# Attention rounds dealt in another way, and three gate tiles of the layer-norm stage computed inside the rounds of the first three head pairs

## The chip, the cores and the metric

The kernel runs on one core of a Trainium2 chip. The metric is device time in microseconds, lower is better; a run's time is that of the whole program.

## What is computed

One inference step of a hybrid encoder layer (depth 1) for two groups that share weights: 1024 new frames of a prompt and 64 new frames of a running stream, 1088 tokens in all, width 1024.

```python
h = rmsnorm(x)
q, k, v, glu_a, glu_b, g_attn, g_conv = split(h @ w_in + b_in)      # 1024 -> 3*512 + 2*512 + 2*1024
q, k = rmsnorm per head (8 heads x 64)
# stick-breaking attention, strictly causal, keys: own frames (+ 2048 cached ones for the sample group)
A[t,s] = sigmoid(z_ts) * prod_{s<j<t} (1 - sigmoid(z_tj));  a = (A @ v) @ w_attn_out
u = glu_a * sigmoid(glu_b);  c = causal depthwise conv of u, width 31, 512 channels
c = silu(layernorm(c)) @ w_conv_out + b_conv_out
x = x + (sigmoid(g_attn) * a + sigmoid(g_conv) * c) @ w_out
x = x + conv_ffn(rmsnorm(x));  y = rmsnorm(x)
```

Keys, values and the convolutions' last rows are outputs too. All of it is in fp32; each product is made of three passes, both factors being split into a high and a low part (`split_passes`).

## The kernel before, in words

PE (TensorE) does the matmuls, ACT (ScalarE) activations and copies out of PSUM, DVE (VectorE) elementwise work, POOL (GpSimd) some subtractions, SP issues the DMAs. Every engine works through its own queue in order; semaphores tie the queues together. The stages are blocks, and at the end of a block the engines meet.

Stage 1 makes `hhi` and `hlo`, the normalised input, and the projections of head pair 0.

Stage 2 is a window for each of the four head pairs p, each of 17 rounds r (0 to 16). A round treats two units of attention: up to 512 keys for 128 queries of one head (rounds 0 to 11; widths 128, 256, 384, 512, then 128 and 512, 256 and 512, 384 and 512, 512 and 512), and from round 12 the 64 sample queries against own and cached keys. A unit goes through the engines so:
- PE: `scores(p, r)` into one of two banks `ZB`;
- ACT: `sig`, two sigmoids per unit, into `sn` (2 buffers) and `sg` (4 buffers). It waits until the scan of the unit two before has read `sn`, and until PE's transposes of the unit four before have read `sg`;
- DVE: `weights`, a scan over `sn` and a product into `sg`;
- PE in round r+2: `w_transposes`; ACT: `w_evac`; PE in round r+3: `outputs`.

Between these pieces PE works on projections for the next pair, in half-jobs ("halves") of 12 matmuls (four of eight contraction tiles, three passes): 9 jobs of the next pair's q, k, v (`qkv_half`, numbers t = 0 to 8, 384 columns) and 6 jobs of its GLU inputs (`ab_half`, 364 columns). The jobs alternate between the two banks `PJ`; a job may start when the job two before it has been evacuated: q, k, v by DVE (`qkv_evac`, semaphore `qkv_ev`), GLU inputs by ACT (`b_evac`, a sigmoid into `sigb`) and DVE (`a_evac`). In each round PE issues scores, outputs of round r-3, masks, all halves but the last, the transposes of round r-2, the last half. The weights of the jobs lie in five slots of `whi` and `wlo`: a DMA fills `wraw`, ACT converts (`slot_hi`), DVE subtracts (`slot_lo`). In the last pair the jobs are 15 chunks of gate tiles 0 to 4 (`gate_half`, evacuated by ACT in `gate_evac`).

DVE also does the 31 taps of the depthwise convolution of pair p (`tap`), dealt over the rounds by the table `TAPS`, one list for each pair; in a round DVE does the evacuation first, then the weights, then `slot_lo` and norms, then its taps. Tap 0 waits until `c_sb` of the pair before has been stored.

Stage 3 computes the other 11 of 16 gate tiles (33 chunk jobs of 24 matmuls on PE, `gate_job`), and beside them the layer norm of the convolution: channel sums, squares, roots, reciprocals, sigmoids, then `chi` (ACT) and `clo` (POOL). ACT and POOL also prepare the weights that follow (`PREP3`, `make_hi`, `make_lo`). Stage 4 reads the gates back from HBM and mixes both branches; it first needs `ohi` and `olo`, made from `oraw`. Stage 5 is the feed-forward network.

Of the kernel before, what the change touches and what calls it, by code (L numbers as in the profile page):

```python
# [15 lines left out]
F32 = mybir.dt.float32  # L16
F32R = mybir.dt.float32r
BF16 = mybir.dt.bfloat16
ALU = mybir.AluOpType
# [3 lines left out]
P = 128  # L23
# [60 lines left out]
def build(nc, a, o, scr):  # L84

    ctx = ExitStack()
    with ctx:
# [27 lines left out]

        def gate_col(g):

            return 3 * AW + 2 * CC + D * (g % 2) + P * (g // 2)
# [24 lines left out]
        gate_ev, gate_out2, c_out, o_out = sem("gate_ev"), sem("gate_out2"), sem("c_out"), sem("o_out")  # L143
        PJ, XB = bank[0:2], bank[2:6]

# [52 lines left out]
        def qkv_evac(dve, p, t):  # L198
# [7 lines left out]
            dve.tensor_tensor(stage[:, t, :], PJ[t % 2][:, 0:3 * P], bqkv[:, :], ALU.add).then_inc(qkv_ev, 1)  # L206

        def qkv_half(pe, p, t, half):
            if half == 0:
                if t == 0:  # L210
                    pe.wait_ge(lo_done, 5 * p + 3)
                if t >= 2:
# [5 lines left out]
            for k in range(4 * half, 4 * half + 4):  # L218
                ws = slice(P * k, P * k + P)
                for n, (x, w) in enumerate(split_passes(hhi, hlo, whi, wlo)):  # L220
                    mm = pe.matmul(PJ[t % 2][:, 0:3 * P], x[:, k, tok], w[:, 0:3, ws],  # L221
# [226 lines left out]
        with ExitStack() as c2:  # L448
# [31 lines left out]
            AB_ROUND = {9: (0, 1), 10: (2,), 11: (3,), 12: (4,), 13: (5,), 14: (6,), 15: (7,), 16: (8, 9, 10, 11)}  # L480
            GATE_ROUND = {r: (2 * r, 2 * r + 1) if r < 13 else (13 + r,) for r in range(NR)}
            B_EVAC_ROUND, A_EVAC_ROUND = {10: 0, 14: 1}, {12: 0, 16: 1}
            NORM_ROUND = {11: 0, 12: 1, 13: 2}
            HI_ROUND, LO_ROUND = {9: 0, 10: 1, 13: 2}, {10: 0, 12: 1, 14: 2}

            def dealt(carried, own):
                out = [[] for _ in range(NR)]
                for p in range(PAIRS):
# [3 lines left out]
                    for r in range(NR):  # L492
# [17 lines left out]
            def _(sp):  # L510
# [41 lines left out]
                def window(p):  # L552
                    load_bias(sp, p + 1)
                    for x in range(2):
                        load_ab(sp, x, p + 1)
# [11 lines left out]
                    load_past(p, 3, "k")  # L567
# [40 lines left out]
            def _(act):  # L608
                def b_evac(p, c):
# [3 lines left out]
                    if later(need):  # L613
                        act.wait_ge(a_ev, need)
                    act.wait_ge(bias_b_done, p + 1)
                    act.activation(sigb[:, 0:c1_ - c0], PJ[(9 + 2 * c) % 2][:, 0:c1_ - c0], ACT.Sigmoid,
                                   bias=bias_b[:, :]).then_inc(b_ev, 1)

# [1477 lines left out]
```

## Time and profile before

| | us |
|---|---|
| median of 3 runs | 1704.54 (1704.46 to 1704.71) |
| profiled execution, its own time | 1699.73 |
| its span | 1697.8 |
| stage 2, windows of the four pairs | 112.6, 116.4, 115.7, 110.0 |
| stage 3 | 137.3 |

The profile comes from one execution, whose time is 4.8 us under the median. Its rows name an engine, a line of the code, and the tile written and those read (out<-in). PE is TensorE's matmul, PEld its weight load, which overlaps. Matmuls are pipelined: one of 384 columns lasts 0.33 us, but the next starts 0.17 us after it, so starts tell more than lengths. An idle time stands in front of the instruction that ended it, with the one that released it. The granted clock is a share of 2.4 GHz.

### The profile page before, as it was taken

The numbers are of one execution on the slowest core, as the hardware profiler recorded it, in microseconds if no ns is written. First come the engines' busy times: TensorE is split into PE (matmuls) and PEld (weight loads), VectorE is DVE, ScalarE is ACT, GpSimd is POOL, SyncE is SP. The second block draws the span as 40 slices with busy tenths as digits, with TensorE's granted clock in tenths as the row PEclk, the third lists the DMA queues.
The fourth block names the chain that finished last, engine by engine and source line by source line (L and its number), as shares of the span: only waits on it lengthen the run. The fifth ranks groups of instructions, "written<-read, shape, count | busy, mean of one in ns | idle before, by whom it ended". The sixth has DMA issues, their size and how long they took to land. (4 is left out here: it accounts for less than half of the span.)

```text
span 1697.8 us, 26678 instructions
## 1 busy us (share of the span) xinstructions
PE 1647.2 (97%) x9802; PEld 1524.0 (90%) x9802; DVE 1131.3 (67%) x1628; ACT 609.3 (36%) x1541; POOL 102.7 (6%) x71
## 2 busy tenths in 40 slices
PE   7999999998999999999999999999999999999998
PEld 6997887887987999999989998999989999998996
DVE  5479799799796233444477665676656666665677
ACT  5446446446444234211154131322313122131224
POOL 0000000000000114332320000000000000000000
PEclk9999999999999999999999999999999999999999
DMA  5330320402313422723312020211102111020102
GB/s 187 84 79 20 93 58 20 126 26 58 92 69 122 157 78 93 242 87 90 102 38 87 26 63 13 62 44 43 49 25 62 33 42 61 25 62 17 57 13 108
DMA packets 145879, 119.42 MB, mean 70 GB/s; under 512 B 6763, under 2 KB 130127, under 8 KB 145800
## 3 DMA queue, kind: packets, MB, share of 16 engines
q1 hardware_dynamic: 145800, 118.35, 22.6%
q8 instruction: 51, 0.84, 0.2%
q14 instruction: 28, 0.23, 0.0%
HBM read 95.83 MB, written 22.50 MB: 70 GB/s over the span
## 5 line engine op out<-in xcount | busy, mean ns | idle before, releaser
L1638 PE MATMUL bank<-h2hi,whi 128*128 128x364 f32 (+1 forms) x1056 | 347.7, 329 | 2.1 <-PEq L1644 2.1
L1638 PE MATMUL bank<-h2lo,whi 128*128 128x364 f32 (+1 forms) x1056 | 347.6, 329 | 0.0
L1638 PE MATMUL bank<-h2hi,wlo 128*128 128x364 f32 (+1 forms) x1056 | 347.5, 329 | 0.0
L1423 DVE TENSOR_TENSOR x<-bank,x 128x512 f32<-128x512 f32 x270 | 181.1, 689 | 166.6 <-PE bank L1413 161.7
L1638 PEld LDWEIGHTS bank<-h2hi,whi 128*128 128x128 f32 x1056 | 199.0, 188 | 2.7 <-issue 2.3
L1638 PEld LDWEIGHTS bank<-h2lo,whi 128*128 128x128 f32 x1056 | 199.0, 188 | 0.4
L1638 PEld LDWEIGHTS bank<-h2hi,wlo 128*128 128x128 f32 x1056 | 199.0, 188 | 0.0
L815 DVE SCALAR_TENSOR_TENSOR c_sb<-u,dww,c_sb 128x1118 f32<-128x1118 f32 x120 | 165.8, 1382 | 2.7
L1413 PE MATMUL bank<-whi,mhi 128*128 128x512 f32 x342 | 133.7, 391 | 2.4 <-PEq L1433 1.2
L1413 PE MATMUL bank<-whi,mlo 128*128 128x512 f32 x342 | 133.3, 390 | 0.0
L1413 PE MATMUL bank<-wlo,mhi 128*128 128x512 f32 x342 | 133.3, 390 | 0.0
L1855 ACT ACTIVATE gsig<-cvg 128x364 f32<-128x364 f32 (+1 forms) x66 | 33.4, 506 | 273.9 <-DVE cvg L1947 273.9
L1163 ACT ACTIVATE whi<-wraw 128x1024 fp32r<-128x1024 f32 x77 | 80.7, 1054 | 89.9 <-PE bank L1413 59.7
L667 ACT ACTIVATE sn<-bank 128x512 f32<-128x512 f32 (+3 forms) x116 | 58.3, 502 | 151.1 <-PE bank L1010 131.0
L221 PE MATMUL bank<-whi,hhi 128*128 128x384 f32 x288 | 103.6, 360 | 5.6 <-DVE stage L206 3.3
L1838 ACT ACTIVATE up<-bank 128x364 f32<-128x364 f32 (+2 forms) x176 | 64.2, 391 | 111.5 <-PE bank L1638 109.4
L221 PE MATMUL bank<-whi,hlo 128*128 128x384 f32 x288 | 99.0, 344 | 0.0
L221 PE MATMUL bank<-wlo,hhi 128*128 128x384 f32 x288 | 98.7, 343 | 0.0
L1363 PE MATMUL bank<-hhi,whi 128*128 128x364 f32 (+1 forms) x264 | 88.0, 333 | 0.9 <-PEq L448 0.9
L1363 PE MATMUL bank<-hlo,whi 128*128 128x364 f32 (+1 forms) x264 | 86.7, 328 | 0.0
L1363 PE MATMUL bank<-hhi,wlo 128*128 128x364 f32 (+1 forms) x264 | 86.7, 328 | 0.0
L1941 DVE TENSOR_SCALAR cvv<-up,ffw,prm 128x364 f32<-128x364 f32 (+1 forms) x66 | 31.0, 470 | 77.0 <-ACT up L1838 77.0
(206 smaller groups left out, 3398.5 us busy)
## 6 DMA issues: line engine op xcount, KB each, us to landing
wraw<-in_w_up SPq DMA_DIRECT2D x88, 256.0 KB, 3.2
wraw<-in_w_in SPq DMA_DIRECT2D x30, 512.0 KB, 5.0
wraw<-in_w_down SPq DMA_DIRECT2D x44, 256.0 KB, 2.8
scr_gate<-gst SPq DMA_DIRECT2D x11, 544.0 KB, 4.4
gch<-scr_gate SPq DMA_DIRECT2D x16, 364.0 KB, 3.7
xt<-in_x_prompt SPq DMA_DIRECT2D x8, 512.0 KB, 5.2
kpast<-in_cache_sb_k SPq DMA_DIRECT2D x16, 256.0 KB, 5.3
wraw<-in_w_out SPq DMA_DIRECT2D x16, 256.0 KB, 2.8
```

Of the source, the lines that this page charges most:

```text
L221: mm = pe.matmul(PJ[t % 2][:, 0:3 * P], x[:, k, tok], w[:, 0:3, ws], start=(k == 0 and n == 0), stop=(k == KT - 1 and n == 2))
L667: act.activation(sn[:, s % 2, 512 - n:512], z, ACT.Sigmoid, scale=-DH ** -0.5)
L815: dve.scalar_tensor_tensor(out=c_sb[:, :], in0=x, scalar=w, in1=c_sb[:, :], op0=ALU.mult, op1=ALU.add).then_inc(tap_done, 1)
L1163: act.activation(dst, wraw[:, parity, :], ACT.Copy).then_inc(sems[1], 1)
L1363: mm = pe.matmul(bank[j % 4][:, 0:c1_ - c0], w[:, g % 5, ws], x[:, k, c0:c1_], start=(k == 0 and i == 0), stop=(k == KT - 1 and i == 2))
L1413: mm = pe.matmul(bank[banks[d % len(banks)]][:, :], x[:, k, TOK[t]:TOK[t] + P], w[:, 512 * half:512 * half + 512], start=(k == 0 and n == ...
L1423: dve.tensor_tensor(y, bank[banks[d % len(banks)]][:, :], y, ALU.add).then_inc(down_ev, 1)
L1638: mm = pe.matmul(bank[(3 * tau + c) % 4][:, 0:c1_ - c0], w[:, ws], x[:, k, c0:c1_], start=(k == 0 and n == 0), stop=(k == KT - 1 and n == 2))
L1838: ins = act.activation(up[:, x, x0 + sh + 2:x1_ + sh + 2], bank[(3 * tau + c) % 4][:, x0 - c0:x1_ - c0], ACT.Copy)
L1855: act.activation(gsig[:, (3 * j + c) % 2, 0:n], cvg[:, c, 0:n], ACT.Sigmoid).then_inc(gsig_done, 1)
L1941: dve.tensor_scalar(dst, src[:, n0 + 2:n1 + 2], w(2), prm[:, ds(PRM_FDB + tile, 1)], ALU.mult, ALU.add).then_inc(c2_done, 1)
```

## The change

- Gate tiles 13, 14 and 15 leave stage 3. Each becomes three chunk jobs (`gate_chunk_half`) inside the window of pair 0, 1 and 2. Stage 3 keeps 8 tiles, 24 jobs.
- The order of jobs in these windows is now q, k, v jobs 0 to 4, gate chunk 0, 5, 6, chunk 1, 7, 8, chunk 2, then the six GLU jobs (`Q_AT`, `GW_AT`). Rounds 3 to 8 hold three halves instead of two, rounds 9 to 11 one instead of two, one and one, rounds 12 and 13 two. In the rounds with cached keys the first half stands ahead of the scores.
- The gate weights use slot 4 and `wraw[0]`; the GLU weights of slot 4 come later, converted in round 9, subtracted in round 10. ACT evacuates gate chunks in rounds 5, 7 and 9, behind `attention(p, r)`, into `sigb`, from which SP stores them.
- DVE's taps are dealt anew, some evacuations come behind the weights, `a_evac`, `b_evac` and the slots move by a round or two.
- The last pair uses the same deal: one half in rounds 9 to 11, three in round 16.
- Stage 3: roots, sigmoids and `chi` move forward by jobs, seven weights are prepared in place of ten, the last behind the last job.

```diff
+        NG = 2 * KT
+        NG3 = NG - 3 - 5
...
+        Q_AT, GW_AT = (0, 1, 2, 3, 4, 6, 7, 9, 10), (5, 8, 11)
...
+                if p and t in (6, 8):
+                    pe.wait_ge(gw_ev, 3 * (p - 1) + t // 2 - 2)
+                elif p and t in (5, 7):
+                    pe.wait_ge(qkv_ev, NT * p + t)
+                elif t >= 2:
                     pe.wait_ge(qkv_ev, NT * p + t - 1)
...
-            AB_ROUND = {9: (0, 1), 10: (2,), 11: (3,), 12: (4,), 13: (5,), 14: (6,), 15: (7,), 16: (8, 9, 10, 11)}
-            GATE_ROUND = {r: (2 * r, 2 * r + 1) if r < 13 else (13 + r,) for r in range(NR)}
-            B_EVAC_ROUND, A_EVAC_ROUND = {10: 0, 14: 1}, {12: 0, 16: 1}
+            LATE_ROUND = {9: (0,), 10: (1,), 11: (2,), 12: (3, 4), 13: (5, 6), 14: (7,), 15: (8,), 16: (9, 10, 11)}
+            B_EVAC_ROUND, A_EVAC_ROUND = {11: 0, 14: 1}, {13: 0, 15: 1}
+            GATE_EVAC_ROUND = {**{n + 1: n for n in range(9)}, 11: 9, 12: 10, 13: 11, 15: 12}
             NORM_ROUND = {11: 0, 12: 1, 13: 2}
-            HI_ROUND, LO_ROUND = {9: 0, 10: 1, 13: 2}, {10: 0, 12: 1, 14: 2}
+            HI_ROUND, LO_ROUND = {11: 0, 12: 1, 14: 2}, {12: 0, 13: 1, 15: 2}
+            GW_FIRST = NG - 3
...
-                         [[3, 2, 1, 1, 3, 2, 2, 2, 3, 2, 0, 0, 0, 0, 1, 3, 6],
-                          [0, 3, 3, 1, 3, 3, 2, 2, 2, 2, 1, 0, 0, 0, 1, 3, 5],
-                          [0, 3, 3, 2, 3, 2, 3, 2, 2, 2, 0, 0, 0, 0, 1, 3, 5],
-                          [0, 3, 3, 3, 3, 3, 2, 2, 3, 1, 3, 3, 2, 0, 0, 0, 0]])
+                         [[4, 1, 1, 2, 4, 4, 4, 3, 4, 1, 0, 0, 1, 1, 1, 0, 0],
+                          [0, 0, 4, 4, 4, 4, 4, 4, 4, 1, 1, 0, 1, 0, 0, 0, 0],
+                          [0, 0, 4, 4, 4, 4, 4, 4, 4, 1, 1, 0, 1, 0, 0, 0, 0],
+                          [0, 0, 4, 4, 4, 3, 2, 2, 3, 0, 1, 1, 3, 3, 1, 0, 0]])
...
-                    for x in range(2):
-                        load_ab(sp, x, p + 1)
+                    load_ab(sp, 0, p + 1)
+                    sp.wait_ge(lo_done, 5 * p + 8)
+                    sp.dma_start(wraw[:, 0, :].rearrange("p (k n) -> p k n", k=KT),
+                                 w_in[:, :, ds(gate_col(GW_FIRST + p), P)]).then_inc(gw_in, 16)
...
+                    sp.wait_ge(gw_lo, p + 1)
+                    load_ab(sp, 1, p + 1)
+                    for c, (c0, c1_) in enumerate(CHUNKS):
+                        sp.wait_ge(gw_ev, 3 * p + c + 1)
+                        sp.dma_start(scr["gate"][GW_FIRST + p][:, c0:c1_], sigb[:, 0:c1_ - c0]).then_inc(gw_out, 16)
                     for s in range(3):
+                        if s == 2:
+                            load_past(p, 3, "k")
                         if p < PAIRS - 2:
                             load_qkv(sp, s, p + 2)
                         else:
                             load_slot(sp, s, 4, gate_col(s))
-                    load_past(p, 3, "k")
...
+                def gate_chunk(p, c):
+                    c0, c1_ = CHUNKS[c]
+                    act.wait_ge(gw_ready, 3 * p + c + 1)
+                    if c or p:
+                        act.wait_ge(gw_out, 16 * (3 * p + c))
+                    if c == 0:
+                        act.wait_ge(a_ev, 3 * p + 3)
+                    act.activation(sigb[:, 0:c1_ - c0], PJ[GW_AT[c] % 2][:, 0:c1_ - c0], ACT.Sigmoid,
+                                   bias=gate_bias(GW_FIRST + p)).then_inc(gw_ev, 1)
...
                     for r in range(NR):
                         attention(p, r)
-                        if r in (0, 1):
-                            slot_hi(act, 3 + r, p + 1)
+                        if r == 0:
+                            slot_hi(act, 3, p + 1)
+                        if r == 1:
+                            gate_weights_hi(p)
+                        if r in (5, 7, 9):
+                            gate_chunk(p, (r - 5) // 2)
+                        if r == 9:
+                            act.wait_ge(gw_ready, 3 * p + 3)
+                            slot_hi(act, 4, p + 1)
...
-                        if 1 <= r <= 13:
-                            gate_evac(r - 1)
-                        if r == 15:
-                            gate_evac(13)
+                        if r in GATE_EVAC_ROUND:
+                            gate_evac(GATE_EVAC_ROUND[r])
...
-                        if 1 <= r <= NT:
+                        if r in (1, 2, 3, 4, 6, 8):
                             qkv_evac(dve, p + 1, r - 1)
                         if r in A_EVAC_ROUND:
                             a_evac(p + 1, A_EVAC_ROUND[r])
                         for u in units_of(r):
                             weights(p, u)
+                        if r in (4, 6, 8):
+                            qkv_evac(dve, p + 1, r)
                         if r == 0:
                             next_bias(p + 1)
-                        if r in (2, 3):
-                            slot_lo(dve, 1 + r, p + 1)
+                        if r == 2:
+                            slot_lo(dve, 3, p + 1)
+                        if r == 3:
+                            dve.wait_ge(gw_hi, p + 1)
+                            dve.tensor_tensor(wlo[:, 4, :], wraw[:, 0, :], whi[:, 4, :].bitcast(F32),
+                                              ALU.subtract).then_inc(gw_lo, 1)
+                        if r == 10:
...
-                        if n == 0:
-                            pe.wait_ge(lo_done, 5 * p + 5)
                         if n < 2:
-                            pe.wait_ge(qkv_ev, NT * p + 8 + n)
+                            pe.wait_ge(lo_done, 5 * p + 4 + n)
+                        if n == 1 and p:
+                            pe.wait_ge(gw_ev, 3 * p)
+                        elif n < 2:
+                            pe.wait_ge(qkv_ev, NT * p + (9 if p else 8 + n))
...
+                def gate_chunk_half(p, c, half):
+                    c0, c1_ = CHUNKS[c]
+                    if half == 0:
+                        if c == 0:
+                            pe.wait_ge(gw_lo, p + 1)
+                        pe.wait_ge(qkv_ev, NT * (p + 1) + 4 + 2 * c)
...
+                    job, half = h // 2, h % 2
+                    if job in Q_AT:
+                        qkv_half(pe, p + 1, Q_AT.index(job), half)
+                    elif job in GW_AT:
+                        gate_chunk_half(p, GW_AT.index(job), half)
                     else:
-                        ab_half(p + 1, (h - 2 * NT) // 2, h % 2)
+                        ab_half(p + 1, job - NT - 3, half)
 
                 def halves_of(p, r):
                     if p == PAIRS - 1:
-                        return GATE_ROUND[r]
-                    return (2 * r, 2 * r + 1) if r < NT else tuple(2 * NT + h for h in AB_ROUND[r])
+                        return (2 * r, 2 * r + 1) if r < NT else tuple(2 * NT + h for h in LATE_ROUND[r])
+                    if r < NT:
+                        return (2 * r, 2 * r + 1) if r < 3 else tuple(range(3 * r - 3, 3 * r))
+                    return tuple(2 * NT + 6 + h for h in LATE_ROUND[r])
 
                 def window(p):
                     for r in range(NR - 1):
                         halves = halves_of(p, r)
+                        if pasts_of(r):
+                            half_(p, halves[0])
...
                     for r in range(NR - 1):
                         halves = halves_of(p, r)
+                        if pasts_of(r):
+                            half_(p, halves[0])
+                            halves = halves[1:]
                         if r < len(ROUNDS):
                             scores(p, r)
...
                     halves = halves_of(p, NR - 1)
                     for x, h in enumerate(halves):
-                        if x == len(halves) - 1:
+                        if x == 2:
                             outputs(p, NR - 3)
+                            if p < PAIRS - 1:
+                                qk_transposes(p + 1, 4)
+                                qk_transposes(p + 1, 5)
                         half_(p, h)
-                        if x < len(halves) - 1:
+                        if x < 2 and p < PAIRS - 1:
                             for n in (2 * x, 2 * x + 1):
...
-            PREP3 = [(g % 5, 3 * (g - 9)) for g in range(10, NG)] + [(1, 21), (2, 24), (3, 27), (4, 30)]
+            PREP3 = [(g % 5, 3 * (g - 9)) for g in range(10, NG3 + 5)] + [(3, 12), (4, 15), (1, 21), (2, 24)]
+            PREP_AT3 = {2: 0, 5: 1, 8: 2, 12: 3, 15: 4, 21: 5, 23: 6}
...
-                    if n in (6, 7, 8):
-                        c_lo(n - 6)
+                    if n == 4:
+                        c_lo(0)
+                        c_lo(1)
+                    if n == 5:
+                        c_lo(2)
...
-                    if j == 15:
+                    if j == 13:
                         roots()
-                    if j in (18, 22, 26):
-                        sigmoids((j - 18) // 4)
-                    if j in (21, 25, 29):
-                        c_hi((j - 21) // 4)
...
+                    if j in (14, 17, 20):
+                        sigmoids((j - 14) // 3)
+                    if j in (16, 19, 22):
+                        c_hi((j - 16) // 3)
+                    if j in PREP_AT3:
+                        n = PREP_AT3[j]
                         act.wait_ge(g_ready, PREP3[n][1])
                         make_hi(act, raw3, n // 2 + 1, n, n % 2, whi[:, PREP3[n][0], :])
...
```

## Rows read from the trace of the kernel before

**Rows 1.** The page, part 1: busy us, share of the span, instructions.
```profile
PE 1647.2 (97%) x9802; PEld 1524.0 (90%) x9802; DVE 1131.3 (67%) x1628; ACT 609.3 (36%) x1541; POOL 102.7 (6%) x71
```

**Rows 2.** By stage: stretch, length, busy PE, PEld, DVE, ACT, POOL; clock, DMA, GB/s.
```profile
91.30:203.90 112.60, 107.73 (x779) 94.60 (x778) 102.53 (x115) 61.50 (x189) 0.00 (x0) 1.00 0.18 51
203.90:320.30 116.40, 109.45 (x778) 96.10 (x778) 102.43 (x115) 61.88 (x189) 0.00 (x0) 0.99 0.22 62
320.30:436.00 115.70, 109.42 (x777) 96.09 (x776) 102.42 (x115) 62.04 (x189) 0.00 (x0) 0.99 0.22 63
436.00:546.00 110.00, 104.52 (x759) 91.01 (x759) 92.16 (x97) 52.99 (x118) 0.02 (x1) 1.00 0.29 92
546.00:683.30 137.30, 136.38 (x812) 134.53 (x813) 42.88 (x36) 48.81 (x69) 37.89 (x15) 1.00 0.34 117
```

**Rows 3.** Waits of PE, 85 to 546 us: who waited for whom, total, times, longest.
```profile
PE bank L960 <- ACT wT L676: 9.6, 8, 2.7
PE bank L999 <- ACT kTpast L683: 6.0, 12, 0.8
PE bank L221 <- DVE stage L206: 3.3, 2, 1.9
```

**Rows 4.** The same view without a filter on the engine.
```profile
ACT sn L667 <- PE bank L1010: 131.0, 47, 4.6
```

**Rows 5.** Timeline of PE, first matmul of stage 4; in brackets the idle time.
```profile
683.31 0.41 PE L1598 MATMUL bank<-chi,whi 128*128 128x364 f32 x1 [0.91 <-PEq L1170]
```

**Rows 6.** Timeline of ACT, the last weight conversion of stage 3.
```profile
678.92 1.05 ACT L1163 ACTIVATE whi<-wraw 128x1024 fp32r<-128x1024 f32 x1
```

**Rows 7.** Timeline of POOL, the subtraction that follows it.
```profile
680.04 2.41 POOL L1167 TENSOR_TENSOR wlo<-wraw,whi 128x1024 fp32r<-128x1024 f32 x1 [4.32 <-ACT whi L1163]
```

**Rows 8.** Landing times of the DMAs that write `oraw`.
```profile
DMA to landing us min/median/max: 4.4/7.2/9.9
```

**Rows 9.** Timeline of ACT, last pair, round 5 of the attention.
```profile
468.52 0.60 ACT L667 ACTIVATE sn<-bank 128x512 f32<-128x512 f32 x1 [4.67 <-DVE run L845]
...
470.45 1.12 ACT L676 ACTIVATE wT<-bank 128x512 f32<-128x512 f32 x2
471.41 0.61 ACT L708 ACTIVATE stage<-bank,prm 128x364 f32<-128x364 f32 x1
```

**Rows 10.** Timeline of DVE, second pair, rounds 2 and 3.
```profile
220.58 0.95 DVE L845 TENSOR_TENSOR_SCAN run<-sn 128x385 f32<-128x385 f32 x1
...
223.50 1.22 DVE L178 TENSOR_TENSOR wlo<-wraw,whi 128x1024 fp32r<-128x1024 f32 x1
224.64 4.22 DVE L815 SCALAR_TENSOR_TENSOR c_sb<-u,dww,c_sb 128x1118 f32<-128x1118 f32 x3
228.77 0.55 DVE L206 TENSOR_TENSOR stage<-bank,bqkv 128x384 f32<-128x384 f32 x1
229.24 1.22 DVE L845 TENSOR_TENSOR_SCAN run<-sn 128x513 f32<-128x513 f32 x1
...
232.97 1.22 DVE L178 TENSOR_TENSOR wlo<-wraw,whi 128x1024 fp32r<-128x1024 f32 x1
```

**Rows 11.** Timeline of PE, second pair, round 5 up to the start of round 6.
```profile
236.03 1.14 PE L979 MATMUL bank<-kT,qT 64*128 64x256 f32 x8
...
240.09 1.04 PE L1010 MATMUL bank<-ident,sg 128*128 128x128 f32 x8
240.88 0.42 PE L221 MATMUL bank<-whi,hhi 128*128 128x384 f32 x1
...
243.17 0.71 PE L979 MATMUL bank<-kT,qT 64*128 64x128 f32 x8
```

**Rows 12.** Timeline of PE after its 1.9 us wait for DVE, second pair.
```profile
230.20 0.52 PE L221 MATMUL bank<-wlo,hhi 128*128 128x384 f32 x1
...
232.75 1.23 PE L1010 MATMUL bank<-ident,sg 128*128 128x128 f32 x6
```

**Rows 13.** Columns as in rows 2 (granted clock third from last), that stretch alone.
```profile
230.00:233.00 3.00, 3.00 (x12) 2.90 (x12) 2.93 (x5) 0.42 (x4) 0.00 (x0) 0.53 0.00 0
```

More of the change, by code:

```diff
@@ L205, in qkv_evac @@
                     dve.wait_ge(wt_ready, NWT * (p - 1) + 6)
-            dve.tensor_tensor(stage[:, t, :], PJ[t % 2][:, 0:3 * P], bqkv[:, :], ALU.add).then_inc(qkv_ev, 1)
+            dve.tensor_tensor(stage[:, t, :], pj_qkv(p, t)[:, 0:3 * P], bqkv[:, :], ALU.add).then_inc(qkv_ev, 1)
         def qkv_half(pe, p, t, half):
@@ L1054, in sample_outputs @@
                     mm.then_inc(av_done, 1)
+                def gate_chunk_half(p, c, half):
[4 more added lines that the diff above has]
+                        pe.wait_ge(qkv_ev, NT * (p + 1) + 4 + 2 * c)
+                    for k in range(4 * half, 4 * half + 4):
+                        ws = slice(P * k, P * k + P)
+                        for i, (w, x) in enumerate(split_passes(whi, wlo, hhi, hlo)):
+                            mm = pe.matmul(PJ[GW_AT[c] % 2][:, 0:c1_ - c0], w[:, 4, ws], x[:, k, c0:c1_],
+                                           start=(k == 0 and i == 0), stop=(k == KT - 1 and i == 2))
+                    if half:
+                        mm.then_inc(gw_ready, 1)
                 def half_(p, h):
@@ L1080, in window @@
                             w_transposes(p, u)
-                        half_(p, halves[-1])
+                        for h in halves[-1:]:
+                            half_(p, h)
                         for j in pasts_of(r + 1):
@@ L1201, in _ @@
                 n = 0
-                for g in range(NG - 5):
-                    while n < len(PREP3) and n < g + 3:
-                        if n < NG - 10:
+                for g in range(NG3):
+                    while n < len(PREP3) and n < g + 2:
+                        if n < NP3:
                             send_raw(sp, raw3, n, n % 2, k_halves(w_in, gate_col(10 + n)))
                         else:
-                            send_out_weights(sp, raw3, n, n % 2, n - (NG - 10), 0)
+                            send_out_weights(sp, raw3, n, n % 2, OUT_ORDER[n - NP3], 0)
                         n += 1
-                    if g == NG - 6:
+                    if g == NG3 - 1:
                         sp.wait_ge(clo_done, 3)
@@ L1283, in _ @@
                 slot_hi(act, 4, 5)
-                for j in range(3 * (NG - 5)):
+                for j in range(3 * NG3):
                     gate_evac(j)
@@ L1370, in channel_mean @@
                     return pe.matmul(bank[4 + c][:, 0:CHUNKS[c][1] - CHUNKS[c][0]], ones[:, :], src, start=True, stop=True)
-                for j in range(3 * (NG - 5)):
+                for j in range(3 * NG3):
                     gate_job(j)
```

43 lines of the change are left out of this document (25 added, 18 removed).

## Prediction

> **What bounds the kernel now.** I read the page's busy table first: PE works 97% of the span [rows 1]. Then the busy time by stage, cut where each head pair's first score matmul starts: the four pair windows last 112.6, 116.4, 115.7 and 110.0 us, the gate and layer-norm stage 137.3 [rows 2]. PE is busy 94% of a pair window and 99% of that stage. So PE's queue sets the time nearly everywhere. Moving matmuls from one stage to another doesn't shorten anything by itself. The change can win only what PE now idles in the pair windows, and it must not add waits there. Third, who waited for whom: over all four pairs PE waited 9.6 us for ACT's copies ahead of the cache transposes, 6.0 us for the transposed cache keys, 3.3 us for DVE's projection evacuation [rows 3]; with smaller items 22 us in all. That is the purse. The opposite direction is the row to look at longest: ACT waited 131.0 us in 47 waits for PE's transposes of the weights [rows 4]. ACT is not busy there, but it is chained to PE: the sigmoids of round r overwrite buffers that PE's transposes of round r-2 must have read, and PE issues these late in round r.
>
> **Part 1, nine gate jobs move.** A job is 24 matmuls. Stage 3 runs 812 matmuls in 137.3 us [rows 2], 0.167 us each, so a job is 4.0 us. Stage 3 falls by 9 x 4.0 = 36.0; the pair windows rise by nine jobs, 36.3 with the slower first matmul after each switch.
>
> **Part 2, the end of stage 3.** Before the change PE's last gate job is followed by an evacuation and a barrier, and stage 4 starts at 683.31 after 0.91 us of idle [rows 5]; the last weight is converted one job earlier and hidden: ACT's conversion 1.05, POOL's subtraction 2.41 [rows 6, 7]. After the change the last of the seven weights is converted on ACT behind the last gate evacuation: 0.6 + 1.05, then 2.41 on POOL, then the barrier, about 4.4 us after PE's last job instead of 1.1: +3.3. The third `clo` part (3.3 us on POOL) also ends only about 1.4 us after PE's last job, so SP's two loads of `oraw` are issued there, land 4.4 us later at best [rows 8], and ACT's `ohi` copies wait for them: about 1.9 us more in front of the second job of stage 4. The layer-norm chain in between (means, squares, roots, reciprocals) keeps two jobs of slack. Stage 3 with its hand-over: -36.0 + 3.3 + 1.9 = **-30.8 us**.
>
> **Part 3, waits on ACT's order.** In rounds 5 and 7 of pairs 0 to 2 the third half-job belongs to projections 6 and 8, which write the PSUM bank that gate chunks 0 and 1 left. It waits for `gw_ev`, and ACT evacuates the chunk only behind `attention(p, r)` of the same round. That call starts with four sigmoids that wait for PE's transposes of that very round, and these stand immediately ahead of the waiting half-job. So PE must sit through four sigmoids, two copies and the evacuation. The last pair has exactly this sequence: first sigmoid at 468.52, copies at 470.45, gate evacuation 471.41 plus 0.61 [rows 9]: 3.5 us, 3.6 with the hand-overs. Round 7 has an `o_sb` copy more (0.5). Cost 3.6 + 4.1 = 7.7 us per pair, 23 us for three. Nothing can hide it, since PE's queue is in order; behind it stand the next round's scores, hence ACT's and DVE's next work.
>
> **Part 4, DVE's deadlines.** DVE is busy 102.4 of 116.4 us in a pair [rows 2] and gets one subtraction more. A tap costs 1.38 (three from 224.64 to 228.77), an evacuation 0.47, a subtraction 1.14, two 384-wide weight units 2.9, two 512-wide ones 3.7 [rows 10]. A PE round with two halves is 7.1 us [rows 11]; a third half adds 2.1 to 2.2. The new deal puts no taps in rounds 0 and 1 of pairs 1 and 2 and four in each of rounds 2 to 8. Walk of pair 1, us from the start of round 2, each line a sum of those prices:
> Round 2: DVE can start its scans at 4.1 (behind PE's scores, one half, transposes and the first sigmoids); 2.9 + 1.1 + 5.5 ends at 13.7. PE enters round 3 at 5.5.
> Round 3: PE wants its third half (projection 4) at 11.8; it needs evacuation 2, which DVE does first in its round 3: 14.2. Stall 2.4 (now 1.9 a round later [rows 3]; the cause there is a tap waiting for a DMA, which the new deal removes). DVE: 0.5 + 3.7 + 1.1 + 5.5, ends 24.6.
> Round 4: PE wants gate chunk 0 at 19.8; its bank needs evacuation 3, done 25.1. Stall 5.3. Round 5 starts at 30.
> Round 5: the ACT-order stall, 3.6. Round 6: evacuation 5, stall 1.3. Round 7: ACT order, 4.1. Round 8: evacuation 7, about 0.8.
> Rounds 9 to 11 now hold one half each, 4.6 to 5.3 us of PE, while DVE comes out of round 8 some 8 us late with 5 to 6 us of work per round: about 2.5 in round 10 (sigmoids behind DVE's scan) and 3.0 in round 11 (slot 4's low part, now made in DVE's round 10, only just before PE needs it); these replace the present 2.7 there. Round 15: 1.2, since the half that covered ACT's last weight copy now stands ahead of the scores.
> New stalls 24; three gate jobs 12; against them the present stall with its slow clock (3.7), 2.7, and some 1.5 from half-jobs ahead of the cache scores and 1 in small items fall away: 24 + 12 - 9 = **+27** for pair 1, and as much for pair 2. Pair 0 has one and two taps in rounds 2 and 3: no stall in round 3, 3.5 in round 4, the rest as before, but also no present stall to lose: **+26**. Pair 3 has no extra jobs; its taps (4, 4, 4 in rounds 2 to 4 against 3, 3, 3) put DVE later, and rounds 9 to 11 give PE less to do meanwhile: walked in the same way 11.2 us of idle for the 5.5 of now, **+5.5**. Pairs: +86 (26 + 27 + 27.5 + 5.5), the third rounded up for its shorter window now.
> The DMAs moved along: the gate weights and three chunk stores per pair on SP have two rounds between them, 15 us for transfers of a few us. The load for slot 0 of the next pair now waits for the late subtraction of round 10 and reaches ACT just in time; bound 0 to 2 us per pair, I take 0.
>
> **Part 5, the clock.** After the 1.9 us wait [rows 3] the granted clock was 0.53 over the next stretch [rows 13], that is the lower level, 1.2 GHz: eight matmuls stand 0.32 us apart instead of 0.17 (230.20 to 232.75), six transposes take 1.23 where eight took 1.04 [rows 11, 12]: 1.2 + 0.4, with the edges 1.7 us lost. The third pair shows the same; the 2.7 us waits of round 11 in three pairs show none. So two of five. Nine stalls of over 3 us are new (rounds 4, 5, 7): 0 to 9 x 1.7 = 15 us, I take two fifths, **+6**. The Trainium skill (TensorE: Matmul & The Clock Gate, section What's actually happening) says that the throttled state is the default and activity releases it. By that each long stall would pay, and the sum would be 9 us higher; the trace agrees only in part.
>
> **Sum.** -30.8 + 86 + 6 = +61. The profiled execution took 1699.7 us (span 1697.8), 4.8 under the median of the runs; against the median 1704.5 + 61 = **1766 us**.
>
> **Rivals.** (A) The sum, 1740 to 1787 with its bounds (clock, slot load, a few us per pair): chance 0.72.
> (B) DVE's deadlines don't bite, because the stalls of part 3 let it catch up each time; only part 3 remains: -30.8 + 36.3 + 23 - 7 (present round-4 stalls) - 4.5 = +17, 1722, spread 1712 to 1739. Against it: round 4 comes before the first such stall, and DVE's 21 us of work in rounds 2 and 3 against 14 of PE's. Chance 0.15.
> (C) The other side: the new jobs fall into PE's present idle time. It decides only if neither part 3 nor part 4 holds, that is, if ACT and DVE are early at every bank. Then -30.8 + 36.3 - 22 = -16.5, 1688 (1680 to 1708 if the purse is only partly emptied). For it: ACT is busy only half of each window [rows 2]. Against: rows 4, idle ACT is not free ACT. Chance 0.05, of which 0.02 within 0.2%.
> (D) The window doesn't grow: weight loads fill only 96.1 of its 116.4 us [rows 2], so 20 us would be open for 12 us of jobs. Then only -30.8: 1674. Against it: transposes and scores follow each other without idle, at 0.79 us for eight [rows 11]; the rest of the load time is theirs. Chance 0.02. The Trainium skill (Perfetto Trace Analysis, section Identifying the Most-Contended Engine) has this as its rule, that PE's headroom is read from weight-load share and not matmul share; it speaks for D.
> (E) Worse: every long stall runs into half clock and the slow PE delays ACT and DVE in turn, +85 to +100, about 1795: 0.06.
> Likeliest time 1766. The range 1716 to 1787 leaves out C, D and E. A change of 0.2% (3.4 us) is about what can be measured. Faster 0.05, within 0.02, slower 0.93.
>
> **What would show it.** Right: stage 3 about 105 us; windows near 139, 143, 143, 115; PE waiting for ACT's gate evacuation (`sigb`) six times for 3.6 to 4.1 us, and for DVE's `stage` evacuation in round 4 of three pairs for 3 to 5; more stretches at half clock. Wrong: pair windows below 130, or no wait on `sigb`, which would break part 3; waits on `stage` missing would make it B.

## The result and the profile after

The changed kernel takes 1772.91 us (median of 4 runs, 1772.42 to 1775.44), beside 1704.5 for the kernel before in the same runs. The ratio of the means is 1.041, interval 1.0396 to 1.0424. The forecast was 1766, with a range of 1716 to 1787. The profiled execution has a span of 1773.6 us, 75.8 more than before. Part 1 of the page, with the columns of rows 1:

```profile
PE 1671.9 (94%) x9802; PEld 1544.1 (87%) x9802; DVE 1129.6 (64%) x1631; ACT 607.2 (34%) x1541; POOL 94.5 (5%) x68
```

PE runs the same 9802 matmuls, yet is busy 25 us longer and idle 51 us longer. Where that lies is told by the stages, cut as in rows 2, with the same columns:

```profile
91.70:237.10 145.40, 128.30 (x851) 113.39 (x850) 103.94 (x116) 63.22 (x193) 0.00 (x0) 0.93 0.16 45
237.10:385.80 148.70, 127.31 (x849) 113.57 (x849) 104.30 (x116) 63.72 (x194) 0.00 (x0) 0.94 0.20 56
385.80:533.40 147.60, 128.79 (x851) 113.50 (x850) 104.29 (x116) 63.75 (x194) 0.00 (x0) 0.93 0.20 57
533.40:652.20 118.80, 105.56 (x760) 91.96 (x759) 92.35 (x97) 53.73 (x119) 0.07 (x1) 0.99 0.29 87
652.20:757.00 104.80, 100.51 (x596) 98.63 (x597) 35.68 (x36) 40.98 (x57) 29.63 (x12) 1.00 0.34 118
```

The pair windows grew by 32.8, 32.3, 31.9 and 8.8 us, 105.8 in all, and stage 3 shrank by 32.5. Each of the first three windows has 72 matmuls more, which are worth 12.1 us; the other 20 us of each are no work. The granted clock fell from 0.99 or 1.00 to 0.93 or 0.94. The waits of PE from 85 to 652 us, as in rows 3:

```profile
PE bank L237 <- ACT sigb L658: 20.8, 6, 3.7
PE bank L1037 <- ACT sg L710: 16.1, 9, 2.8
PE bank L1123 <- DVE stage L218: 12.4, 4, 3.8
PE bank L1110 <- ACT wT L718: 5.9, 4, 1.5
PE bank L978 <- DVE wlo L190: 5.1, 3, 2.8
PE bank L237 <- DVE stage L218: 4.5, 2, 2.2
```

L237 is a matmul of a projection, L1123 of a gate chunk, L1037 a score, L978 an A or B half-job, L1110 an output from cached values. In idle times of more than 0.15 us PE has stood still for 70 us up to the end of stage 3 instead of 23, +47. So of the 105.8 us, 36.3 are the moved matmuls, 47 are waits, and 22.5 are left. They lie in how fast PE goes after a wait. The second pair, round 4, timeline of PE:

```profile
268.47 0.34 PE L237 MATMUL bank<-whi,hlo 128*128 128x384 f32 x1
272.52 0.64 PE L1123 MATMUL bank<-hhi,whi 128*128 128x364 f32 x1 [3.71 <-DVE stage L218]
272.96 0.51 PE L1123 MATMUL bank<-hlo,whi 128*128 128x364 f32 x1
273.27 0.51 PE L1123 MATMUL bank<-hhi,wlo 128*128 128x364 f32 x1
```

and the stretch behind it, columns as above:

```profile
272.60:278.60 6.00, 6.00 (x22) 5.92 (x23) 0.83 (x3) 1.15 (x5) 0.00 (x0) 0.50 0.00 0
```

PE stands 3.71 us, then starts a matmul each 0.30 us instead of 0.17, at a granted clock of 0.50, that is 1.2 GHz. In stage 2 the records show 61.4 us at this level, against 6.8 before: 54.6 more, and the 22.5 us left over are 0.41 us for each of them. This is a remainder, not a measurement. It can be held against another reading of the same trace: 5.0 of the 61.4 us lie inside waits, and if PE works at half speed in the other 56.4, it loses 28.2 us there, against 3.4 before. That is 24.8 more, an estimate near the 22.5.

### The profile page after: what moved, and what is told of

Its sections match the earlier page's. It is cut to its first block and busy times, and to the rows that moved or that the text cites. A ratio compares the mean times of both kernels' runs of the same rounds, so it can differ in the third digit from the quotient of the medians.

```text
span 1773.6 us, 26704 instructions
## 1 busy us (share of the span) xinstructions
PE 1671.9 (94%) x9802; PEld 1544.1 (87%) x9802; DVE 1129.6 (64%) x1631; ACT 607.2 (34%) x1541; POOL 94.5 (5%) x68
## 5 line engine op out<-in xcount | busy, mean ns | idle before, releaser
L237 PE MATMUL bank<-whi,hhi 128*128 128x384 f32 x288 | 106.0, 368 | 27.6 <-ACT sigb L658 20.8
L893 DVE TENSOR_TENSOR_SCAN run<-sn 128x129 f32<-128x129 f32 (+3 forms) x68 | 54.3, 799 | 77.1 <-ACT sg L710 77.1
L237 PE MATMUL bank<-whi,hlo 128*128 128x384 f32 x288 | 101.6, 353 | 0.0
L237 PE MATMUL bank<-wlo,hhi 128*128 128x384 f32 x288 | 101.3, 352 | 0.0
L237 PEld LDWEIGHTS bank<-whi,hhi 128*128 128x128 f32 x288 | 57.7, 201 | 31.6 <-ACT sigb L658 22.3
L1499 PEld LDWEIGHTS bank<-whi,mhi 128*128 128x128 f32 x342 | 64.2, 188 | 15.8 <-issue 3.1
```

The costliest lines, as they stand in the source:

```text
L237: mm = pe.matmul(pj_qkv(p, t)[:, 0:3 * P], x[:, k, tok], w[:, 0:3, ws], start=(k == 0 and n == 0), stop=(k == KT - 1 and n == 2))
L893: dve.tensor_tensor_scan(run[:, s % 3, 512 - n:513][:, ::-1], x, x, init, ALU.mult, ALU.min).then_inc(scan_done, 1)
L1499: mm = pe.matmul(bank[banks[d % len(banks)]][:, :], x[:, k, TOK[t]:TOK[t] + P], w[:, 512 * half:512 * half + 512], start=(k == 0 and n == ...
```

## Experiments

All compare with the kernel before on the same chip (1702 to 1704 us) and show the ratio to it; the changed kernel's is 1.041. Experiments 1 to 4, 5 to 8, 9 to 11, and 12 ran on four different chips, so between these groups the ratios tell more than the microseconds.

**1 to 3: which engine holds PE up.** Theory A: each stall of the prediction is a term of its own. Theory B: DVE paces the stretch, and the wait for ACT only stands ahead of one for DVE. First, ACT takes the gate chunk ahead of the attention work:

```diff
                     for r in range(NR):
+                        if r in (5, 7, 9):
+                            gate_chunk(p, (r - 5) // 2)
                         attention(p, r)
...
-                        if r in (5, 7, 9):
-                            gate_chunk(p, (r - 5) // 2)
```

> The changed kernel (1772.9 us), with one edit: in rounds 5, 7 and 9 ScalarE evacuates the gate chunk ahead of the round's attention work instead of behind it. Theory A (each stall is its own term): the six waits of TensorE for sigb in rounds 5 and 7, 20.8 us in the changed kernel's profile, go, and the stretches at half clock behind them with them, some 7 us: about 1745 us. Theory B (VectorE, with four taps in each of rounds 2 to 8, paces the whole stretch, and the ScalarE wait only stands ahead of a VectorE wait that would come anyway): TensorE waits for stage or for w_done instead, in rounds 6 to 8, and at most 5 us are won: about 1768 us. Above 1757 is B, below is A.

Measured 1774.9 us, ratio 1.0428 (1.0402 to 1.0454): nothing won. PE's waits, 85 to 652 us:

```profile
PE bank L1123 <- DVE stage L218: 36.7, 9, 4.6
PE bank L1037 <- ACT sg L710: 14.0, 7, 2.8
PE bank L978 <- DVE wlo L190: 8.2, 3, 2.8
```

The 20.8 us for `sigb` in rounds 5 and 7 are gone, and the waits of the gate chunks for DVE rose from 12.4 in 4 to 36.7 in 9: beside round 4's 3.7 now 4.6 in round 6 and 3.0 to 4.5 in round 8. The waits moved one round on and changed their name. Second, DVE takes tiles 3, 5 and 7 behind the weights of the round that computes them, ahead of its four taps (5.5 us):

```diff
-                        if r in (1, 2, 3, 4, 6, 8):
+                        if r in (1, 2, 3):
                             qkv_evac(dve, p + 1, r - 1)
...
-                        if r in (4, 6, 8):
+                        if 3 <= r <= 8:
                             qkv_evac(dve, p + 1, r)
```

> The changed kernel, with one edit: in rounds 3 to 8 VectorE evacuates the projection tile of the round behind the round's running products and ahead of its taps, instead of tiles 3, 5 and 7 at the head of the next round. Theory A: the waits of TensorE for stage in round 4 (12.4 us in 4) shrink to under 2 us, the half clock behind them goes too, and the ScalarE waits of rounds 5 and 7 stay as they are: about 1756 us. Theory B: VectorE is merely handed its work in another order, its taps push the running products of the next round back, and TensorE meets ScalarE's and VectorE's lateness a round later: 1765 us or more.

Measured 1757.9 us, ratio 1.032 (1.029 to 1.035), as A said: the waits of round 4 went, the 20.8 us for `sigb` stayed. Third, both edits:

> The edits of the two experiments before it together. Theory A (independent terms): their gains add, some 28 + 16 us: about 1729 us. Theory B (one chain paced by VectorE): together hardly more than the better of the two: 1755 us or more. If the two together bring more than their sum, each had only moved the stall to the other engine.

Measured 1729.3 us, ratio 1.0162 (1.0133 to 1.0192): 43.7 us less than the changed kernel, where the edits alone gave nothing and 15. The waits for `sigb` are gone and those of the gate chunks for DVE's `stage` with them; what is left, 85 to 605 us:

```profile
PE bank L1037 <- ACT sg L710: 14.5, 9, 2.8
PE bank L237 <- DVE stage L218: 9.0, 5, 2.2
```

The time is the one that A forecast, but not by A's addition: the first edit alone had brought nothing, and brings 28.6 us once the second is in. That is the last sentence of the expectation. Round 4's wait was DVE's alone. In rounds 5 to 8 DVE's queue and ACT's order are two chains that end at nearly the same moment, and each alone suffices to hold PE. The stretches at half clock fell from 61.4 to 23.9 us with them.

**4: the last pair.** Its rounds, evacuations and taps are dealt as in the kernel before; in part:

```diff
-                        return (2 * r, 2 * r + 1) if r < NT else tuple(2 * NT + h for h in LATE_ROUND[r])
+                        return (2 * r, 2 * r + 1) if r < 13 else (13 + r,)
...
-                          [0, 0, 4, 4, 4, 3, 2, 2, 3, 0, 1, 1, 3, 3, 1, 0, 0]])
+                          [0, 3, 3, 3, 3, 3, 2, 2, 3, 1, 3, 3, 2, 0, 0, 0, 0]])
```

> The changed kernel with the last pair's rounds, evacuations and taps dealt as in the kernel before. The prediction put +5.5 us on the last pair; its stretch has since measured 118.8 us against 110.0. Theory A: all of the 8.8 us is the new deal of that pair: 1764 us. Theory B: part of it comes from the pair ahead (the carry-over of taps, the state of the clock) and stays: 1768 to 1772 us.

Measured 1767.6 us, ratio 1.038 (1.0352 to 1.0407). The window is 115.6 us: 3.2 of the 8.8 us came back. The time is close to B's, but the rest does not come from the pair ahead. Rounds 0 to 11 now take 73.8 us against 74.2 in the kernel before, and the pair's waits for sigmoids are 0.8 us instead of 8.5; but some 5 us of other waits stand in rounds 12 to 15, where this kernel, having one half-job in each, still put it ahead of the scores and left nothing behind the transposes. In experiment 8, which undoes that among other things, the window is 109.6.

**5: the clock.** Twenty matmuls of 384 columns are put ahead of the last half-job of rounds 4 and 5. In round 5 that is the half-job that waits. In round 4 it isn't: there the second of the three half-jobs waits, and the fillers stand behind that wait:

```diff
+                        if r in (4, 5) and p < PAIRS - 1:
+                            filler(p, r)
                         for h in halves[-1:]:
                             half_(p, h)
```

> The changed kernel plus 20 matmuls of 384 columns (some 3.4 us of work, results never read, into a bank that is free then) just ahead of the half-job that waits in rounds 4 and 5 of the first three pairs: TensorE works where it stood idle. If the half clock in the rounds behind those two waits comes from the standing still, the stretches at half clock in stage 2 (61 us in the profile of the changed kernel) shrink by a third or more and the time falls by 5 to 12 us, although 120 matmuls more are done: 1761 to 1768 us. If the clock falls for another reason, the filler only takes the place of the waits where they are at least as long, and lengthens the rest: 1773 to 1780 us.

Measured 1778.1 us, ratio 1.0441 (1.0427 to 1.0455): slower, in the range of the second reading. The half clock fell from 61.4 to 47.8 us, by 22%, where the first reading asked for a third. PE's waits, 80 to 655 us, then the second pair's round 4, with the fillers in its last row:

```profile
PE bank L1123 <- DVE stage L218: 15.0, 7, 3.7
PE bank L1037 <- ACT sg L710: 14.4, 8, 2.8
PE bank L237 <- ACT sigb L658: 11.2, 3, 3.7
```

```profile
273.30 0.64 PE L1123 MATMUL bank<-hhi,whi 128*128 128x364 f32 x1 [3.67 <-DVE stage L218]
...
276.66 0.82 PE L1068 MATMUL bank<-ident,sg 128*128 128x128 f32 x6
277.23 3.72 PE L1132 MATMUL bank<-hhi 128*128 128x384 f32 x20
```

In round 5 the fillers took the wait away in all three pairs, and no slow stretch lies there any more, where two of three had one. Instead a wait of 1.15 us for DVE stands in round 6 of each, where only pair 1 had one. In round 4 the wait of 3.7 us comes first and the fillers after it, so it could not shrink: those 60 matmuls were work for nothing. So 120 matmuls of 0.172 us cost 20.6 us, 11.5 us of waits went, and 13.6 us of half clock are worth 5.6 at 0.41. The sum is 3.5; the profiled span changed by 1.4, the median by 5.2. Half of the cost is the misplaced half, 10.3 us, so the run doesn't show whether fillers that stand only where PE waits would pay. In round 5 it does show a PE that doesn't stand still and keeps its clock.

**6: taps.** Only the taps are spread; the rows of pairs 1 and 2, and pair 0's in the same manner:

```diff
-                          [0, 0, 4, 4, 4, 4, 4, 4, 4, 1, 1, 0, 1, 0, 0, 0, 0],
+                          [0, 1, 2, 2, 3, 3, 3, 3, 3, 2, 0, 0, 0, 0, 1, 3, 5],
```

> The changed kernel with nothing but the taps of the first three pairs spread more evenly: at most three in a round, and eight of them in the last two rounds, where VectorE stands idle for 12 us. Theory A (independent terms): what TensorE waits for VectorE in rounds 3, 4, 8 and 10 goes (some 22 us of waits with 5 us of half clock), the ScalarE waits of rounds 5 and 7 stay: about 1747 us. Theory B (the two engines stand in for each other, as moving the ScalarE evacuation alone showed): the ScalarE waits remain whole and set the pace of rounds 5 to 8, so that only the waits of rounds 3, 4 and 10 go: about 1758 us.

Measured 1758.6 us, ratio 1.033 (1.0315 to 1.0344), the time of B, though not by all of its steps. The waits for `sigb` are 20.8 us to the digit. Those of round 3 are gone, those of round 10 are at most 1.1 us instead of 2.5; round 4's is 2.3 in pair 0 and still 3.6 in the others, since tile 3 is evacuated only at the head of DVE's round 4 there. And PE, now earlier in round 11, waits 4.2 us for `wlo`, slot 4's low part, in pairs 1 and 2.

**7: the kernel before, lightened.**

```diff
-                          [0, 3, 3, 1, 3, 3, 2, 2, 2, 2, 1, 0, 0, 0, 1, 3, 5],
-                          [0, 3, 3, 2, 3, 2, 3, 2, 2, 2, 0, 0, 0, 0, 1, 3, 5],
+                          [0, 2, 2, 1, 3, 3, 3, 3, 2, 2, 1, 0, 0, 0, 1, 3, 5],
+                          [0, 2, 2, 1, 3, 3, 3, 3, 2, 2, 1, 0, 0, 0, 1, 3, 5],
...
-                        if r == 10:
+                        if r == 11:
                             roots(p + 1)
...
-            NORM_ROUND = {11: 0, 12: 1, 13: 2}
+            NORM_ROUND = {12: 0, 13: 1, 14: 2}
```

> The kernel before, without any gate tile in the pairs, with two edits: one tap less in rounds 1 and 2 of pairs 1 and 2 (moved to rounds 5 and 6), and the square roots with the two table loads of ScalarE one round later, where it stands idle, the norms one round later with them. In its profile TensorE waits 9.6 us for wT evacuations (three of them 2.7 us, behind the square roots) and 3.3 us for stage tiles, with 6.8 us at half clock behind the latter. If both go: 12 to 15 us less, about 1690 us. If the waits are only passed on to the next round: 1698 to 1703 us.

Measured 1718.1 us, ratio 1.0083 (1.0069 to 1.0097): both expectations missed. Its first wait of PE, and SP's issues in the second pair:

```profile
PE bank L1052 <- DMA vpast<-in_cache_sb_v: 14.2, 3, 4.8
```

```profile
313.62 0.67 SPq L540 DMA_DIRECT2D out_v_sample<-stage  x1
314.35 1.40 SPq L531 DMA_DIRECT2D vpast<-in_cache_sb_v  x1
```

The stores of keys and values wait for the norms. Norms a round later put the load of past values behind them in SP's queue: its issue lies 104.4 us behind the start of the window (209.9), where it lay 100.0 behind it before, and PE waited 4.8 us for a transfer that takes 3.9. The kernel shows 27.3 us at half clock, 20.5 of them at these three.

**8: every cure.** Experiments 3, 4 and 6 together, tile 2 evacuated in its own round, the later roots of 7, and for the last pair:

```diff
-                        if pasts_of(r):
+                        if pasts_of(r) and p < PAIRS - 1:
                             half_(p, halves[0])
```

> The changed kernel with every cure at once: ScalarE evacuates the gate chunks first, VectorE evacuates each projection tile behind the running products of its own round, the taps are spread (at most three in a round), the square roots stand a round later, and the last pair is dealt as before, its half-jobs too. The gate tiles stay inside the pairs. By the sum, the 36 us of matmuls that are moved and the 36 us that stage 3 loses cancel, 5 us of hand-over and start of stage 4 remain, and 10 us of waits of the kernel before go with the square roots and the spread taps: about 1700 us. If the rounds that carry three half-jobs cost of their own more than their matmuls, it stays above 1710 us.

Measured 1733.9 us, ratio 1.0179 (1.0165 to 1.0193). The intervals of this and of experiment 3 overlap, so the further cures brought nothing, where the expectation was 1700 us. Two waits stand in the way: 15.3 us for `vpast`, again outside DVE and ACT, and 10.9 for `wlo`, which DVE makes.

**9 to 11: the queue.** Two edits to 8, of which the second alone is applied to 7; the third kernel is 8 with the first edit and the old roots:

```diff
-                        if r == 10:
+                        if r == 9:
                             slot_lo(dve, 4, p + 1)
...
-                    store_kv(p + 1)
                     for j in (2, 3):
                         load_past(p, j, "v")
+                    store_kv(p + 1)
                     store_o(p)
```

> The kernel with every cure (1733.9 us) and two edits: the low part of the A weights is made in round 9 instead of round 10, and SyncE issues the loads of the past values ahead of the stores of keys and values. Its profile shows TensorE waiting 15.3 us for vpast (three times 5) and 10.9 us for wlo (three times 3.6). Theory A (SyncE stands at the store, which waits for the norms that the later square roots pushed back, and the loads stand behind it): both waits go with most of the half clock behind them, 1704 us. Theory B (the transfers themselves are late, or the stores in their turn hold up the next pair's first evacuation): the waits move to the first rounds of the next pair, 1720 us or more.

> The kernel before with one tap less in rounds 1 and 2 and the later square roots (1718.1 us), and now the loads of the past values ahead of the stores of keys and values in SyncE's queue. Theory A: the 14.2 us of waits for vpast and the 20 us more of half clock go, and what remains is the gain that was forecast first: 1692 us. Theory B (the stores come late in their turn, or the square roots cost as much a round later): 1700 to 1706 us.

> As the first kernel of this group, but the square roots in round 10 and the order of SyncE's queue as they were in the changed kernel: gate tiles inside the pairs, evacuations early, taps spread, low part of the A weights in round 9, last pair as before. If the square roots and the queue are a wash, it is level with the first kernel, about 1705 us; if the later square roots are worth their 8 us, some 1712 us.

Measured 1716.7 (ratio 1.0095, 1.0080 to 1.0111), 1698.2 (0.9982, 0.9973 to 0.9991) and 1706.9 us (1.0029, 1.0017 to 1.0042). The first two lie between what their theories forecast. The third comes to the 1705 of its expectation, but is not level with the first kernel: it is 10 us below it. The waits for `vpast` are gone in the two in which SP's order changed and, but for 0.5 us, in the third, in which the norms are early again: either end of the mechanism removes them. The waits for `wlo` went with the earlier low part. In the first kernel these stand in their place:

```profile
PE bank L1017 <- ACT wT L718: 12.0, 11, 3.1
...
PE bank L237 <- issue: 4.5, 3, 2.1
```

The later square roots stand ahead of copies that the cache transposes need, and 2.1 us appear in the first rounds of each following pair, as theory B had it. In 10 too `wT` costs 9.5 us, as much as in rows 3. The roots in round 10 are the better place. The stages of experiment 11, the first three pairs and the last:

```profile
90.00:216.50 126.50, 121.07 (x851) 108.01 (x850) 104.00 (x116) 63.00 (x193) 0.00 (x0) 0.99 0.18 52
216.50:345.00 128.50, 120.81 (x851) 107.58 (x850) 104.04 (x116) 63.62 (x194) 0.00 (x0) 0.99 0.23 65
345.00:474.90 129.90, 121.93 (x851) 108.84 (x850) 104.19 (x117) 63.66 (x194) 0.00 (x0) 0.97 0.22 64
474.90:584.40 109.50, 104.39 (x759) 90.97 (x758) 92.29 (x98) 53.40 (x119) 0.00 (x0) 1.00 0.30 95
```

The gate tiles are still inside the pairs, with DVE as busy as in the changed kernel. The windows are those of rows 2 plus 12.1 us for the three jobs, to within 2.1. Its profiled span is 7.3 us over the kernel before's: 3.4 in the windows, 3.4 of idle time ahead of stage 4, 1.3 from there to the end, 0.3 of slower first matmuls, less 1.3 ahead of stage 2; rounding leaves 0.2. Between the medians it is 4.8. So of the 4.1% that the change cost, 0.3% are left with the gate tiles still in the pairs: the loss lay in the order of the work beside them.

**12: a kernel below both.** The kernel before with the taps of 7, the roots left in round 10, and one high-part copy moved:

```diff
-            HI_ROUND, LO_ROUND = {9: 0, 10: 1, 13: 2}, {10: 0, 12: 1, 14: 2}
+            HI_ROUND, LO_ROUND = {9: 0, 11: 1, 13: 2}, {10: 0, 12: 1, 14: 2}
```

> The kernel before with one tap less in rounds 1 and 2 of pairs 1 and 2, the square roots left in round 10, and only the high-part copy that stands behind them (1.05 us of ScalarE) moved from round 10 to round 11, where ScalarE has 2.9 us free. Theory: the 3.3 us of waits for stage go with the 6.8 us at half clock behind them, and each of the three waits of 2.7 us behind the square roots shrinks by about 1 us: 1694 to 1697 us, below both kernels. Rival: as with the later square roots, what is freed is paid again a round later, and the time is within 0.2% of the kernel before (1699 to 1705 us).

Measured 1695.4 us, ratio 0.9955 (0.9942 to 0.9968). Waits of PE, 80 to 550 us, to be read against rows 3:

```profile
PE bank L960 <- ACT wT L676: 7.2, 8, 2.0
PE bank L999 <- ACT kTpast L683: 5.8, 12, 0.8
PE bank L920 <- DVE stage L206: 2.5, 2, 1.4
```

The wait for `wT` is 2.4 us smaller (the longest 2.0 for 2.7). That for `stage` passed from the projections of round 4 to the first B half-jobs of round 9, and is 0.8 smaller. So the time is the one forecast, by half of its reasons: the three long waits shrank by 0.7 to 0.9 us each, but neither the wait for `stage` nor the half clock went. The profiled execution has 10.2 us at that level, and its span is only 2.1 us under the one before, so how the 7 us between the medians divide is open.

## Why the prediction held, and where it did not

**Part 1**, nine jobs: 812 matmuls in stage 3 became 596, of which each window shows 72. Right.

**Part 2**, the end of stage 3. The first matmul of stage 4, to be read against rows 5:

```profile
757.01 0.64 PE L1684 MATMUL bank<-chi,whi 128*128 128x364 f32 x1 [4.31 <-PEq L1254]
757.45 0.51 PE L1684 MATMUL bank<-clo,whi 128*128 128x364 f32 x1
757.76 0.51 PE L1684 MATMUL bank<-chi,wlo 128*128 128x364 f32 x1
```

The idle time is 4.31 for 0.91, +3.4 where 3.3 was summed. The stage with it lost 32.5 us. The 1.9 us more at the start of stage 4 came, as 25.97 us for its first 144 matmuls instead of 24.01, but mostly not from where the prediction put them: for `olo` PE waited 0.4 us. The other 1.5 us are slow matmuls: after 4.31 us of idle they follow each other at 0.30 us instead of 0.17. The size was right by accident, the mechanism wrong.

**Part 3**, ACT's order: six waits of 3.6 and 4.1 were forecast, six came, 3.2 us in round 5 and 3.7 in round 7, 20.8 for 23. As waits they were read rightly. As a price they can't be read: experiment 1 removed them and won nothing. The sum didn't need that, since the prediction walked parts 3 and 4 as one order of events; but its 7.7 us per pair are not what a cure of part 3 would bring.

**Part 4**, DVE's deadlines. Round 3: 2.2 in pairs 1 and 2, forecast 2.4. Round 4: 3.7 in all three, forecast 5.3 in pair 1 and 3.5 in pair 0. Round 6: 1.2 in one pair, forecast 1.3 in each. Rounds 10 and 11: 2.5, and 1.2 to 2.8, forecast 2.5 and 3.0. Round 15: 1.5, forecast 1.2. Round 8's 0.8 did not show. In all, the walk gave +50 of windows beyond the moved matmuls, and +47 of waits came. (The terms listed for pair 0 add up to 26.9 and not 26.) The windows came out longer than forecast all the same: 145, 149, 148 and 119 us for 139, 143, 143 and 115, and part 5 says why. That DVE's queue is the cause of these waits is shown twice. Experiment 6 changes only the taps and takes 14 us away, though round 4's wait stays at 3.6 us in two pairs; experiment 2 hands the tiles over ahead of the taps, and round 4's wait goes with 15 us. The last pair lost 8.8 us for the 5.5 forecast, with 13.2 us of idle time for the 11.2 walked; one of its waits, of 2.8 us, has a slow stretch.

**Part 5**, the clock, is the term that was mis-sized: +6 was taken, within 0 to 15, and some 22 us came. Three steps failed. The share of long stalls that end in half clock was taken as two of five, from waits of 1.5 to 2.7 us; of the nine stalls of 3.2 us and more eight had a slow stretch at their end. Stalls under 3 us were not counted; of the seven of 2.2 to 2.8 us six had one too, even both of 2.2 us in round 3. And the loss of one was taken as 1.7 us from a single stretch, while behind four of the long stalls the slow stretch was twice as long as behind the rest. Fourteen of sixteen stalls thus have one, while the three of 2.7 us of the kernel before have none; what sets them apart no run shows. The Trainium skill (TensorE: Matmul & The Clock Gate, section What's actually happening) says that the slow state is the default and that activity lifts it. Read so that every long stall pays, it agrees with fourteen of sixteen here and not with those three. The prediction had weighed that reading at 9 us more and set it aside for the two fifths; it would have been nearer.

**The rivals.** B, that DVE's deadlines don't bite, falls by the 12.4 and 4.5 us of waits for `stage`. C and D fall by the windows: weight loads fill 113.4 of 145.4 us, and yet no job went into the rest. Even in experiment 11, where PE waits 24 us in stage 2 against 22 in the kernel before, these windows are longer by the 12.1 us of their jobs or more, with weight loads in 107.6 of 128.5 us. Of E the first half came, half clock behind nearly every long stall, but as 68 us and not 85 to 100; that the slow PE delays ACT and DVE in turn no run shows.

**The number.** The sum was 61, and the two profiled executions, from which its terms were read, differ by 75.8. The nearly 15 missing are the clock's 16 less some 3 of waits walked too long, and about 1 in small items. The medians differ by only 68.4, because the profiled execution of before lay 4.8 us under its median and that of the changed kernel 2.5 over its own. So the forecast came out 7 us low and not 15, and that half of its nearness is luck.

## What to carry to other kernels

Waits that an in-order engine shows in a row may be two chains that end together: removing one then wins nothing (0 us here), and what the other brings (15) tells nothing of both (44). So a wait's length is no price until one knows which event comes next behind it. And on the queue of an engine that only issues transfers, whatever waits for a moved step holds up every load behind it: square roots and norms one round later cost 14 us of waits for cached values that nobody had thought of. A filler against idle time has to be checked in the timeline before its time is read: in experiment 5 half of them stood on the wrong side of the wait.

## What the runs showed of the hardware

A wait can cost PE more than its length. All nine waits of 3.0 to 4.6 us for DVE in experiment 1 have a slow stretch at their end, and so have the three for `vpast` in experiment 7; the three of 2.7 us in the kernel before [rows 3] have none, though waits of 2.2 us elsewhere do, and even its two of 1.9 and 1.5 us for `stage`. Over stage 2 of the changed kernel the loss was about 0.41 us for each microsecond at half clock, 22 us for 55. A PE kept at work through the wait (experiment 5, round 5) kept its clock in all three pairs, where two of three had lost it.
